# A hybrid decoder step on one Trainium2 core: top-256 keys by a 32-round bitwise threshold search instead of 32 rounds of MAX8, with the plan of the steps around it re-placed

## What is computed

```python
h = rmsnorm(xp, attn_norm_g)
q, k, v, iq, ik, iw, gq, gk, gv, gr, la = project(h, w_in, ...)
dots = einsum('bqhd,bsd->bqhs', iq, idx_keys)          # indexer, 8 heads
score = einsum('bqh,bqhs->bqs', iw, relu(dots))        # float32
score = where(key_pos <= t_pos, score, -inf)
_, sel = lax.top_k(score, topk)                        # 256 of up to 2048 keys a row; equals: the earlier key
... softmax attention over the kept keys, with a relative bias ...
g_o, S = gla_chunked(gq, gk, gv, la, s0)               # gated linear attention, chunks of 64
x = x + concat(attn_o, gla_readout(g_o, gr)) @ w_out
x = x + (silu(rmsnorm(x) @ w_gate) * (rmsnorm(x) @ w_up)) @ w_down
y = rmsnorm(x)
```

## Time and profile before

| what | value |
|---|---|
| time, median of 3 runs | 4444.63 us (4441.96 to 4448.02) |
| the profiled execution's own time | 4443.38 us |
| its span | 4441.6 us |
| PE busy | 3334.8 us (75%) |
| DVE busy | 2531.8 us (57%) |
| ACT, POOL busy | 1192.0 us, 1077.5 us |
| MAX8, 465 of them (line 1439) | 651.7 us |
| MATCH_REPLACE8 (line 1441) | 644.2 us |
| granted clock of PE, mean | 0.863 |

### The profile page before, as it was taken

One profiled execution on the slowest core, in us unless ns is written; L12 is line 12 of the kernel. 1 busy time (PEld: TensorE's weight loads), 2 busy tenths in 40 slices (PEclk: granted clock), 3 DMA queues, 4 the chain that ended last, 5 costly groups with the idle time before them and its releaser, 6 DMA issues.

```text
span 4441.6 us, 67462 instructions
## 1 busy us (share of the span) xinstructions
PE 3334.8 (75%) x26714; PEld 2689.3 (61%) x26714; DVE 2531.8 (57%) x4016; ACT 1192.0 (27%) x2002; POOL 1077.5 (24%) x979
## 2 busy tenths in 40 slices
PE   6867477778987878888677957879657889167687
PEld 3656245666666767676566646666546676156577
DVE  3537158645852397238953498534997247996100
ACT  2334123333323221323132301333112324012211
POOL 0233113123612332133112222122310123010142
PEclk8978678789998989999798978889878899678889
DMA  4335344344634433243214332143312143011244
GB/s 155 117 126 186 100 129 144 119 154 137 230 127 140 131 122 125 96 150 125 78 56 152 113 105 85 49 148 108 124 59 66 62 165 125 32 60 52 86 148 147
DMA packets 200573, 514.20 MB, mean 116 GB/s; under 512 B 20242, under 2 KB 79458, under 8 KB 200130
## 3 DMA queue, kind: packets, MB, share of 16 engines
q1 hardware_dynamic: 200258, 509.88, 35.3%
HBM read 443.67 MB, written 66.15 MB: 115 GB/s over the span
## 4 chain that ended last, share of the span: by engine, by line
PE 29%; DVE 19%; issue 18%; DVEq 15%; POOLq 7%; ACT 4%; POOL 3%; DMA 2%; SPq 1%; ACTq 0%
DVEq L1442 11%; DVE top L1439 10%; PE bank L763 6%; PE bank L764 6%; PE bank L765 6%; PE bank L812 3%; DVE T L1462 2%; ACT T L1362 2%; DVEq L1440 2%; PE bank L801 1%; POOLq L1793 1%; DMA FR<-in_xT 1%; DVE T L1441 1%; DVE ring L1429 1%; PE bank L788 1%
## 5 line engine op out<-in xcount | busy, mean ns | idle before, releaser
L763 PE MATMUL bank<-FR,ring 128*128 128x256 f16 (+1 forms) x4224 | 1199.2, 284 | 42.5 <-DVE ring L1429 23.9
L764 PE MATMUL bank<-FR,ring 128*128 128x256 f16 (+1 forms) x4224 | 1197.5, 284 | 0.0
L765 PE MATMUL bank<-FR,ring 128*128 128x256 f16 (+1 forms) x4224 | 1195.3, 283 | 0.0
L1439 DVE MAX8 top<-T 128x8 f32<-128x384 f32 (+14 forms) x465 | 651.7, 1402 | 34.0 <-POOL T L1933 4.2
L1441 DVE MATCH_REPLACE8 T<-top,T 128x384 f32<-128x384 f32 (+14 forms) x465 | 644.2, 1385 | 1.2 <-issue 1.2
L788 PE MATMUL bank<-kT,q 128*128 128x256 f16 (+3 forms) x384 | 134.7, 353 | 513.4 <-DVE mx L1462 489.6
L763 PEld LDWEIGHTS bank<-FR,ring 128*128 128x128 f16 x4224 | 428.6, 101 | 121.8 <-issue 20.0
L764 PEld LDWEIGHTS bank<-FR,ring 128*128 128x128 f16 x4224 | 425.2, 101 | 74.5 <-issue 1.7
L765 PEld LDWEIGHTS bank<-FR,ring 128*128 128x128 f16 x4224 | 425.1, 101 | 73.8
L788 PEld LDWEIGHTS bank<-kT,q 128*128 128x128 f16 x384 | 44.0, 115 | 588.8 <-DVE mx L1462 552.6
L763 PE MATMUL bank<-T,ring 128*128 128x256 f16 (+3 forms) x1280 | 372.9, 291 | 35.0 <-DMA ring<-halves_kept 17.5
(11 more groups left out here) (285 smaller groups left out, 5622.4 us busy)
## 6 DMA issues: line engine op xcount, KB each, us to landing
ring<-halves_kept SPq DMA_DIRECT2D x605, 512.0 KB, 3.5
halves_kept<-ring SPq DMA_DIRECT2D x93, 512.0 KB, 5.1
ring<-halves_kept SPq DMA_DIRECT2D x52, 384.0 KB, 3.4
kT<-in_w_gu SPq DMA_DIRECT2D x33, 512.0 KB, 6.1
kT<-in_w_in SPq DMA_DIRECT2D x18, 512.0 KB, 6.7
ikT<-in_w_gu SPq DMA_DIRECT2D x17, 512.0 KB, 5.9
T<-in_xT SPq DMA_DIRECT2D x8, 1024.0 KB, 6.8
FR<-in_xT SPq DMA_DIRECT2D x8, 1024.0 KB, 8.4
```

The lines of the kernel that those rows point to most:

```text
L763: mm(o, lhs[0], rhs[0], start=first, stop=False)
L764: mm(o, lhs[0], rhs[1], start=False, stop=False)
L765: return mm(o, lhs[1], rhs[0], start=False, stop=last)
L1439: v.max(top8[rows, :], view)
```

## The change

The threshold of a row, the 256th largest score, is found bit by bit. A candidate float is kept as an integer of 32 bits; a round counts how many scores of the row are at or above the candidate, starting the sum from −256, so that the sign of the sum says whether the bit stays; three one-element integer instructions make the next candidate. 32 rounds settle 32 bits. `keep_top` then counts the scores above the threshold, numbers the equal ones with a running sum that starts from that count, drops the equal ones past 256, and writes the mask. The sample tokens' picks stay with MAX8.

`E_NARROW`, `E_WIDE`, `HEAD_USES` and the weights in `attention_steps` change, `YS`/`YR` move among the `O` uses, and block 1 gets a step `LOADS` of its own, ahead of `IS0`, in which SP issues the sample loads.

```diff
-ROUNDS = TOPK // 8
+ROUNDS = 32
...
-E_NARROW = {1: ["E1"], 2: ["E2", "FS"], 3: ["E3", "FR"], 4: ["E4"], 5: ["E5"], 6: ["GA"], 7: ["GC0"], 8: ["GC1", "OUTP"],
-            10: ["GD1"], 12: ["GD2"]}
-E_WIDE = {3: ["E1"], 5: ["E2"], 6: ["E3"], 9: ["E4"], 10: ["E5"], 11: ["GA"], 12: ["GC0"], 13: ["GC1", "OUTP"],
-          14: ["GSA"], 15: ["GSB"], 16: ["GSN0", "GSN1"], 17: ["GSN2", "GSN3"], 18: ["GSN4", "GSN5"],
-          19: ["GSN6", "GSN7"], 22: ["GD1"], 24: ["GD2"]}
-HEAD_USES = 4
+E_NARROW = {1: ["E1"], 2: ["E2"], 3: ["E3", "FS"], 4: ["E4"], 5: ["E5", "FR"], 8: ["GA"], 9: ["GC0"], 10: ["GC1", "OUTP"],
+            11: ["GD1"], 12: ["GD2"]}
+E_WIDE = {3: ["E1"], 5: ["E2"], 7: ["E3"], 9: ["E4"], 11: ["E5"], 13: ["GA"], 14: ["GC0"], 15: ["GC1", "OUTP"],
+          16: ["GSA"], 17: ["GSB"], 18: ["GSN0", "GSN1"], 19: ["GSN2", "GSN3"], 20: ["GSN4", "GSN5"],
+          21: ["GSN6", "GSN7"], 23: ["GD1"], 24: ["GD2"]}
+HEAD_USES = 6
...
-        out.append((("IS0", b), 3.0))
-        out += [(("IS", b, s), 1.0) for s in range(DB)]
+        out.append((("LOADS", b), 60.0))
+        out.append((("IS0", b), 5.0))
+        out += [(("IS", b, s), 1.5) for s in range(DB)]
...
-        out += [(("AS", b, s), 3.0) for s in range(DB)]
+        out += [(("AS", b, s), 5.0) for s in range(DB)]
...
-        return ("K", b, i, r), 2 * 128 * (i + 1) / 960.0 + 0.3
+        return ("K", b, i, r), 128 * (i + 1) / 960.0 + 0.6
...
-        return max(0.3, keys * 1.6e-3 + 1.2 - keys * 0.84e-3 - (i + 1) * 0.22)
+        return max(0.3, 2.5 - keys * 1e-3)
...
-        out.append((("KE", b, i0), 0.5))
-        late = [pick(i1, r) for r in range(ROUNDS)]
+        out.append((("KE", b, i0), 6.5 * 128 * (i0 + 1) / 960.0))
+        late = [(step, w - 0.4) for step, w in (pick(i1, r) for r in range(ROUNDS))]
...
-                out.append((("KE", b, i1), 0.5))
+                out.append((("KE", b, i1), 3.0 * 128 * (i1 + 1) / 960.0))
...
-            steps += [("O", b - 1, k) for k in range(len(o_uses(b - 1)))]
+            uses = [("O", b - 1, k) for k in range(len(o_uses(b - 1)))]
+            half = len(uses) // 2
             if b >= 2:
-                steps += [("YS", b - 2), ("YR", b - 2)]
+                steps += [("YS", b - 2)] + uses[:half] + [("YR", b - 2)] + uses[half:]
+            else:
+                steps += uses
             steps.append(("XF", b - 1))
...
+        bits = sb("bits", [128, 2 * ROUNDS + 2], I32)
+        tries = sb("tries", [128, 4], I32)
+        reach = sb("reach", [128, 2])
...
+        marks = T[:, 11776:12800].bitcast(F16)
...
+                    sp.dma_start(bits[:, :], a["bits"]).then_inc(S("bits_in"), 16)
...
-                if kind == "IS0":
+                if kind == "LOADS":
                     for who in ENG:
                         sp.wait_ge(S("bar_" + who), BARS[at - 1] + 1)
...
+            def search_round(view, r):
+                keys = view.shape[1]
+                cand, back, ahead = (tries[:, j:j + 1] for j in range(3))
+                v.tensor_scalar(marks[:, 0:keys], view, cand.bitcast(F32), -float(TOPK), ALU.is_ge, ALU.add,
+                                accum_out=reach[:, 0:1])
+                v.tensor_tensor(ahead, cand, bits[:, ROUNDS + r:ROUNDS + r + 1], ALU.bitwise_xor)
+                dve.drain()
+                v.tensor_scalar(back, reach[:, 0:1].bitcast(I32), bits[:, 2 * ROUNDS:2 * ROUNDS + 1], bits[:, r:r + 1],
+                                ALU.arith_shift_right, ALU.bitwise_and)
+                dve.drain()
+                v.tensor_tensor(cand, ahead, back, ALU.bitwise_xor)
+                dve.drain()
+
+            def keep_top(view):
+                keys = view.shape[1]
+                m = marks[:, 0:keys]
+                cut_at = tries[:, 0:1].bitcast(F32)
+                v.tensor_scalar(m, view, cut_at, 0.0, ALU.is_gt, ALU.add, accum_out=reach[:, 1:2])
+                dve.drain()
+                v.tensor_scalar(m, view, cut_at, None, ALU.is_equal)
+                dve.drain()
+                v.tensor_tensor_scan(m, m, m, reach[:, 1:2], ALU.add, ALU.max)
+                dve.drain()
+                v.tensor_scalar(m, m, float(TOPK), None, ALU.is_gt)
+                dve.drain()
+                v.scalar_tensor_tensor(m, view, cut_at, m, ALU.is_equal, ALU.mult)
+                dve.drain()
+                v.scalar_tensor_tensor(view, m, TAKEN, view, ALU.mult, ALU.add)
+                dve.drain()
+                v.tensor_scalar(view, view, cut_at, OUTSIDE, ALU.is_lt, ALU.mult)
...
-                    pick_round(slice(0, 128), row_of(i))
+                        if i == 2:
+                            dve.wait_ge(S("bits_in"), 16)
+                        v.memset(tries[:, 0:1], 0)
+                        dve.drain()
+                    search_round(row_of(i), r)
                 if kind == "KE":
-                    picked(row_of(step[2]))
+                    keep_top(row_of(step[2]))
                     dve.drain().then_inc(S("a_picked"), 1)
```

More of the change, by code:

```diff
@@ L112, in constants, with search_bits @@
     return c, rep.reshape(64, -1), np.concatenate([hot1, hot2], 1)
+def search_bits():
+    back = [0xFFFFFFFF] + [1 << (31 - r) for r in range(1, ROUNDS)]
+    ahead = [1 << (30 - r) for r in range(ROUNDS - 1)] + [0]
+    bits = np.array(back + ahead + [31, 0], np.uint32).view(np.int32)
+    return np.repeat(bits[None, :], 128, 0)
 def near_chunks(i):
@@ L692, in _ @@
                         for who in ENG:
-                            sp.wait_ge(S("bar_" + who), BARS[at - 2 - len(o_uses(0))] + 1)
+                            sp.wait_ge(S("bar_" + who), BARS[AT["PR", 1] - 1] + 1)
                     else:
@@ L2012, in laid_out @@
         "rel_bias": np.asarray(i["rel_bias"]),
-        "consts": cst, "rep": rep, "hots": hots,
+        "consts": cst, "rep": rep, "hots": hots, "bits": search_bits(),
     }
```

## The result

The changed kernel takes **4371.9 us** (median of 4 runs, 4369.6 to 4378.8) against 4443.3 for the kernel before: 0.9842 of its time, 95% interval 0.9825 to 0.9859. So it is faster by 71 us (1.6%), inside the range of the prediction, but less than half of the 164 us forecast. The profiled execution took 4378.8 us, its span is 4377.0.

A forecast was written before the change was run, and what follows sets the result against it. DVE was taken to bound the searches of blocks 3 to 7, PE heads and tails. Terms −113 − 111 + 52 − 4 − 8 − 4 + 24 = −164 us against 4443.4 gave 4279 us, range 4185 to 4395.

The forecast's parts named there:

- Rival one: In each search round, the counting pass runs at two keys per 1.04 ns, giving 4079 us; chance 0.12.
- the shortest row: Mask's running sum priced by the shortest profiled instance, 2.1 ns a key; both masks together then cost 106 us.
- the mean row: Mask's running sum priced by the profile's mean instead, 4.9 ns a key; both masks would cost 147 us.
- the xor: In a round, the xor between accumulator read and drain counted as hidden under that wait; unhidden it adds 0.1 us.
- 0.16 for the last one: The round's last one-element instruction taken as 0.16 us of the 0.97 us fixed part.
- rival two: Small instructions slowed at the round's serial end: fixed part 2.2 us, 4720 us; decides from 1.42 us on; chance 0.09.
- the 15%: Second searches: only 85% of the 131 us of DVE time gained was counted, 111 us.
- the seven `D` uses: Seven `D` uses of blocks 3 to 7 move behind the last round into the tail, 7.4 us each: +52 us.
- some 143 of DVE: Block 7's second search: PE's 114 us set against some 143 of DVE, so DVE stays the bound.
- rival three: PE becomes the bound of the second searches; DVE's gain there is 59 instead of 111 us, 4331 us; chance 0.15.
- the wait at the eighth `P` use: In the head, `FR` on DVE ahead of the eviction of `P6` makes PE wait a new 5 us.
- The three old waits: PE's head waits at `YR`, `FR` and `GA`: 6.5 of 7.2, 2.6 and 9.3 us go, 18.4 a block.

The follow-up runs named there:

- Two small instructions: The changed kernel with each round's three one-element instructions cut to two, both tensor-scalar with per-partition operands: 4317.7 us, ratio 0.9724.
- the new weights alone: The changed kernel with only the planner's weights altered (first round by 1.4, units by 0.4, second mask by 0.5): 4312.0 us, ratio 0.9713.
- the halves: `FR` cut in two on DVE, behind the evictions of `P6` and `P7`, replacing early `FR` in the 4179.3 us kernel with other repairs, 4 head uses, new weights: 4125.0 us.
- the dealt loads: The changed kernel with four sample page loads behind each `U` use and the wider ones between the sample index's steps: 4338.5 us, ratio 0.9774.

## Why the prediction was right and wrong

**The round: right where POOL is quiet.** The counting pass takes 2345 ns at 2048 keys and a round of 1920 keys 2.97 us wherever POOL is quiet, the forecast's numbers. Rival one fell.

**The mask: right.** At 1920 keys it takes 14.4 us, as priced, and its running sum 4217 ns, 2.1 ns a key: the shortest row was the right one, the mean row was not. Block 7's first tile, parts of it:

```profile
3823.22 2.21 DVE L1486 TENSOR_SCALAR_CACHE_REDUCE T<-T,tries 128x1920 f16<-128x1920 f32 x1
...
3826.81 4.22 DVE L1490 TENSOR_TENSOR_SCAN T<-T,reach 128x1920 f16<-128x1920 f16 x1
...
3836.38 1.22 DVE L1498 TENSOR_SCALAR T<-T,tries 128x1920 f32<-128x1920 f32 x1
```

**First searches: −113 forecast, −64 measured.** The step that failed is in the fixed part of the round: "the xor ... I count as hidden", "0.16 for the last one", from rows of one-element instructions that were "steady at 0.16". Those rows are instructions with one input. Two of the round's three have two inputs from SBUF and stand behind POOL: 47 us in 160 rounds, 0.3 us a round, so a fixed part of 1.27 in place of 0.97 in these stretches, over the 1.2 that the prediction had named as a sign of being wrong. That is the mechanism of rival two, from another cause, in a size below the 1.42 from which it would have decided. Two small instructions brought 40 of these 47 back in the first searches.

**Second searches and tails: −59 forecast, −64 measured.** Here the sum held, in part by luck. Cut at the last round, the rounds of the second tiles gave 150 us where the forecast has 166 (186 less the 15%, 20 us), and the stretches behind them grew by 85 us where the masks (55) and the seven `D` uses (52) make 107: two misses that cancel. The `D` uses in the tail do cost their time, as the new weights alone show; how much of the masks is hidden was not tried. The "some 143 of DVE" that the prediction has for block 7 is the length of the stretch: DVE's own 170.3 us less 54 for the rounds and plus 14 for a mask make 130, and 128.0 were measured, with PE at 110.2, so PE was nearer than it said. DVE is still the busier of the two, and rival three did not come in the changed kernel.

**Heads: −4 forecast, +19 measured.** The failing step is "`YS` goes ahead of the `O` uses and `YR` between them, so ... 6.5 of the 7.2 us go". The wait at `YR` did go; but the step counted PE, DVE and POOL, and left out SP, which it moves too: SP waits at `YR` for y, with only the tiles of the first O uses and five more behind it issued. PE's waits for a tile rose by 18 us over the five heads, from 13 to 31, where the sum has nothing. The second step is a term that was too small: the wait at the eighth `P` use was foreseen (5 us) and is 7.4 to 8 in blocks 2 to 7, 10 in block 1; over the five heads 40 us in place of 25. The barrier behind the head took 4 us more. The three old waits went as forecast, by 91 us (92). Against these stands that the ten more `U` uses made PE's busy time longer by 36 us and not by 53, beside a mean granted clock of 0.93 after 0.92; why by so little is not shown.

**Blocks 0 to 2: +12 forecast, +45 measured.** Block 2: the sum moved seven D uses of blocks 3 to 7 into the tail and forgot block 2's two, some 18 us (9.1 each, as they have 320 columns); its tail, in which the longer second mask stands too, grew from 84 to 109 us. Block 1: the wait on PE came, 47 us where some 35 were said; the stages up to its first search cost 35 us, as forecast (31 and 3), but its searches and tail gave back 2 in place of 10, since the tail grew by 7; why is not shown. Block 0's 5 us are no effect that the runs can show.

So the causes of the miss are shown by runs for the first searches (two small instructions), for SP (the store behind the `O` uses) and, with other repairs in place, for `FR` at the eighth `P` use (the halves). That block 2's two uses cost their full time is read off the trace; under the new weights they left its tail and block 2 lost 18 us, but other uses moved with them. Block 1's 9 us stay open: what the dealt loads brought back is the wait that the forecast had.

## What to carry to other kernels

A one-element instruction on DVE is only cheap if it can't be held up: with two inputs from SBUF it may stand for a whole instruction of POOL, so small serial steps should take their second operand as a per-partition scalar. When a step moves in a plan, follow every queue that walks it, the one that issues DMAs too: a wait there delays all the loads behind it. When an engine's work gets shorter, the planner's weights decide where the other work goes; uses left in a stretch that is PE's cost their full time, and a long piece of work between two evictions is hidden best in pieces shorter than what PE holds in its two banks.

## What was not expected of the hardware

One-element tensor-tensor instructions of 0.15 us took up to 1.20 us, and each of the 159 late ones ended within 18 ns of the end of an instruction on POOL; the tensor-scalar form beside them never moved from 0.27. And a wait of PE can cost more than its length: behind 5.6 us of waiting the granted clock was 0.87 for 12 us, while behind the wait of 1.5 us at the head's start it was 1.00. So moving the store, which took 32 us of PE's idle time out of the heads, gave 43.
